# A hybrid mixing block with a mixture of experts: low parts and rotations to VectorE, convolution to GpSimd, modulation rows split over two stages

## What is computed

```python
mod = silu(c) @ w_ada + b_ada                      # 1024 -> 6 x 1024
sh1, sc1, gt1, sh2, sc2, gt2 = split(mod, 6)
h = rms_norm(x, g_mix_pre) * (1 + sc1) + sh1
proj = h @ w_in                                    # 1024 -> 3148 columns
mq, mk, mv, mo, mi, mf, aq, ak, av, iq, ik, iw = split(proj)
mq, mk = split(silu(causal_conv([mq, mk], conv_w, conv_b)))   # 4 taps, 1024 channels
hm = sigmoid(mo) * head_norm(mlstm(mq, mk, mv, mi + b_igate, mf + b_fgate))
ik = layer_norm(ik); aq, ak, iq, ik = partial_rope(...)
ha = attention over the 128 keys with the highest indexer score, causal by chunks of 64
x = x + gt1 * rms_norm([hm, ha] @ w_out, g_mix_post)
h2 = rms_norm(x, g_ffn_pre) * (1 + sc2) + sh2
x = x + gt2 * rms_norm(moe(h2), g_ffn_post)        # 64 experts, 8 per token, one shared
```

## Time and profile before

| | us |
|---|---|
| median of 3 runs | 1194.58 |
| lowest, highest | 1193.11, 1201.09 |
| the profiled execution | 1198.99 |
| its span in the profile | 1197.2 |
| DVE busy in the span | 841.9 |
| PE busy in the span | 1047.7 |
| POOL busy in the span | 408.4 |

### The profile page before, as it was taken

The page is one execution under the profiler, slowest core; times in us unless marked ns, Lnnn a source line. Parts: engine busy times, 40 slices in busy tenths (PEclk is TensorE's granted clock), DMA queues, the critical chain, the costliest instruction groups (busy, mean ns, idle before and its releaser), DMA issues. The chain is left out here.

```text
span 1197.2 us, 16021 instructions
## 1 busy us (share of the span) xinstructions
PE 1047.7 (88%) x4777; PEld 747.3 (62%) x4778; DVE 841.9 (70%) x1425; ACT 527.1 (44%) x615; POOL 408.4 (34%) x195
## 2 busy tenths in 40 slices
PE   1698997778999979999999999999999999899960
PEld 1595987735744745666666776666666666566630
DVE  4786999955624283888788887867777686676735
ACT  3323263245412113555555554554555454454522
POOL 1342495100000021454453664333434252243322
PEclk9797998878999789999999999999999899899985
DMA  9664344150040737999999999999999999999843
GB/s 358 237 216 139 101 148 142 36 194 1 1 186 6 292 122 274 378 360 334 349 348 364 339 350 322 346 340 335 329 339 333 343 341 303 319 329 315 299 103 150
DMA packets 84489, 302.93 MB, mean 253 GB/s; under 512 B 10997, under 2 KB 23329, under 8 KB 74921
## 3 DMA queue, kind: packets, MB, share of 16 engines
q1 hardware_dynamic: 70336, 263.30, 60.9%
q0 software_dynamic: 12544, 35.70, 12.9%
q10 hardware_dynamic: 1514, 2.97, 0.7%
HBM read 276.80 MB, written 27.30 MB: 254 GB/s over the span
## 5 line engine op out<-in xcount | busy, mean ns | idle before, releaser
L1720 DVE TENSOR_TENSOR w_gate_up_lo<-side,w_gate_up_hi 128x2048 fp32r<-128x2048 f32 x64 | 146.7, 2294 | 82.9 <-ACT w_gate_up_hi L1637 82.7
L1720 DVE TENSOR_TENSOR w_gate_up_lo<-main,w_gate_up_hi 128x2048 fp32r<-128x2048 f32 x64 | 146.7, 2293 | 79.6 <-ACT w_gate_up_hi L1637 79.6
L1637 ACT ACTIVATE w_gate_up_hi<-side 128x2048 fp32r<-128x2048 f32 x64 | 122.2, 1910 | 116.0 <-DMA side<-in_w_exp_up 65.7
L1637 ACT ACTIVATE w_gate_up_hi<-main 128x2048 fp32r<-128x2048 f32 x64 | 122.2, 1910 | 108.3 <-DMA main<-in_w_exp_up 53.5
L1801 PE MATMUL ps<-w_gate_up_hi,xT_hi 128*128 128x512 f32 x512 | 146.4, 408 | 13.2 <-DVE xT_lo L1724 10.2
L1480 POOL DMA_INDIRECT xg<-h_rows,row_numbers x48 | 98.6, 2055 | 173.6 <-issue 128.0
L1801 PE MATMUL ps<-w_gate_up_hi,xT_lo 128*128 128x512 f32 x512 | 139.4, 395 | 0.0
L1801 PE MATMUL ps<-w_gate_up_lo,xT_hi 128*128 128x512 f32 x512 | 138.8, 394 | 0.0
L1486 POOL DMA_INDIRECT y_rows_even<-yb,row_numbers x32 | 79.7, 2490 | 103.4 <-issue 103.4
L1801 PEld LDWEIGHTS ps<-w_gate_up_hi,xT_hi 128*128 128x128 f32 x512 | 93.2, 192 | 34.2 <-issue 15.7
L1801 PEld LDWEIGHTS ps<-w_gate_up_hi,xT_lo 128*128 128x128 f32 x512 | 97.4, 190 | 21.5
(11 more groups left out here) (294 smaller groups left out, 1751.8 us busy)
## 6 DMA issues: line engine op xcount, KB each, us to landing
side<-in_w_exp_gate SPq DMA_DIRECT2D x60, 512.0 KB, 9.9
side<-in_w_exp_up SPq DMA_DIRECT2D x60, 512.0 KB, 24.5
main<-in_w_exp_gate SPq DMA_DIRECT2D x60, 512.0 KB, 10.3
main<-in_w_exp_up SPq DMA_DIRECT2D x60, 512.0 KB, 23.5
side<-in_w_ada SPq DMA_DIRECT2D x24, 1024.0 KB, 6.9
side<-in_w_exp_down SPq DMA_DIRECT2D x16, 1024.0 KB, 24.8
main<-in_w_exp_down SPq DMA_DIRECT2D x16, 1024.0 KB, 25.0
maskb<-in_w_exp_down SPq DMA_DIRECT2D x16, 1024.0 KB, 23.9
```

The lines of the kernel that those rows point to most:

```text
L1637: nc.scalar.activation(whi[:, half], wgu[n % RING][:, :, HALF * half:HALF * (half + 1), :] .rearrange("p m c f -> p c m f"), ACT.Copy).the ...
L1720: nc.vector.tensor_tensor(wlo[:, half], src, whi[:, half].bitcast(F32), ALU.subtract).then_inc(s_wlo, 1)
```

## The change

- In-projection: low parts and rotations move from POOL to VectorE, the low parts into the rounds of the selection at places written in `low_at`. The convolution's three later taps move from VectorE to POOL, each as a product with a scalar (into the place of the result, `qkc`) and a sum; three buffers hold taps instead of two.
- The gates' work and the query turns move from the attention stage into the in-projection: turns on TensorE, scans on VectorE between rounds, exponentials and copies on ScalarE.
- TensorE's order: item 0 goes over h's chunks in the outer loop, with the low weight part second; item 3's four tiles are put between the indexer's turns and products.
- Of the four later rows of `mod` only two (8 pieces) are summed here. One piece of the third is loaded in the attention stage, seven pieces are loaded in the output stage; VectorE sums them there, four ahead of the first tile, three after the tiles and one before the routing. The row sums of TensorE are split: four halves after `scores(0)`, two after `project_out(0)`, two before the last small product.

`gates(1)` is the five instructions L846 to L850, `gates(2)` the six L870 to L877, with the same shapes (4 x 512). `modulate(n)` is `modulation` with the stage's own buffers; `products(i)` and `relu_products(i)` are the loops over heads at L670 and L416 for one i; `early_rows(a, b)` is `modulation` for those pieces.

```diff
-ROWS = [("row", s, q) for s in range(2, 5) for q in range(4)]
-LAST_ROW = [("last", 5, q) for q in range(4)]
+ROWS = [("row", s, q) for s in range(2, 4) for q in range(4)]
-STREAM = (ADA + ITEMS[0:2] + ROWS[0:2] + ITEMS[2:3] + ROWS[2:5] + ITEMS[3:5] + ROWS[5:7] + ITEMS[5:6] + ROWS[7:8] + ITEMS[6:8]
-          + LAST_ROW[0:1] + ITEMS[8:9] + LAST_ROW[1:2] + ITEMS[9:10] + ROWS[8:9] + LAST_ROW[2:3] + ITEMS[10:] + LAST_ROW[3:4]
-          + ROWS[9:])
+STREAM = (ADA + ITEMS[0:2] + ROWS[0:2] + ITEMS[2:3] + ROWS[2:4] + ITEMS[3:4] + ROWS[4:7] + ITEMS[4:5] + ROWS[7:8] + ITEMS[5:])
...
+            for c in range(2 * HEADS):
+                pool.wait_ge(s_tap, c + 1)
+                o, r, x = taps[c % 3], raw[:, c % 4, :], qkc[:, c, :]
+                for j in range(1, CONV):
+                    step(nc.gpsimd.tensor_scalar(x, r[:, j:j + SEQ], cols[:, 8 * j + c:8 * j + c + 1], None, ALU.mult))
+                    ins = nc.gpsimd.tensor_tensor(o, o, x, ALU.add)
+                    step(ins) if j < CONV - 1 else ins.then_inc(s_conv, 1)
...
+            copy_nat(3, [0, 1])
+            for i in range(1, NT):
+                relu_products(i)
+                if i + 1 < NT:
+                    copy_nat(3, [i + 1])
...
+                if c >= 3:
+                    silu_qk(c - 3)
+                first_tap(c)
                 if c % 2:
                     high_part(7 + c // 2)
...
-                        ins = nc.scalar.activation(w, w, ACT.Copy, scale=cs[:, 2 * q + b:2 * q + b + 1])
...
+                if c == 1:
+                    act.wait_ge(s_absf, 1)
+                    step(nc.scalar.activation(gt, gt, ACT.Exp, scale=-1.0))
+                    nc.scalar.activation(gt, gt, ACT.Ln, bias=1.0).then_inc(s_lse, 1)
+                if c == 5:
+                    act.wait_ge(s_em, 1)
+                    nc.scalar.activation(gt, gt, ACT.Exp, scale=-1.0).then_inc(s_emd, 1)
...
+            silu_qk(7)
             copy_nat(10)
-            silu_qk(7)
+            for h in range(HEADS + 1):
+                act.wait_ge(s_qT, h + 1)
...
+            def low_part(m):
+
+                n = KC * width(ITEMS[m])
+                dve.wait_ge(s_whi, m + 1)
+                nc.vector.tensor_tensor(wlo[:, m % 2, 0:n], stage[:, place[ITEMS[m]] % SLOTS, 0:n],
+                                        whi[:, m % 2, 0:n].bitcast(F32), ALU.subtract).then_inc(s_wlo, 1)
...
+            low_part(0)
             dve.wait_ge(s_mod, 1)
...
+            low_part(1)
             dve.wait_ge(s_bias, 48)
...
+            early_rows(0, 2)
+            low_part(2)
+            early_rows(2, 4)
...
+            rope(IQ0, IH, IDIM, ROT_I, K_COSI, K_SINI, None)
+            rope(IK0, 1, IDIM, ROT_I, K_COSI, K_SINI, s_rope)
+            early_rows(4, 7)
+            low_part(4)
+            early_rows(7, 8)
...
+            low_at = {(1, 1): 5, (1, 11): 6, (1, 15): 7, (2, 1): 8, (2, 8): 9, (2, 15): 10, (3, 8): 11}
+            gates_at = {(1, 14): 1, (2, 0): 2}
+            rope_at = (1, 10)
...
-                    if (i, r) in conv_at:
-                        conv(conv_at[i, r])
+                    if (i, r) == rope_at:
+                        dve.wait_ge(s_natd, first[5])
+                        rope(AK0, 1, DH, ROT_A, K_COSA, K_SINA, None)
+                        rope(AQ0, HEADS, DH, ROT_A, K_COSA, K_SINA, s_roped)
+                    if (i, r) in gates_at:
+                        gates(gates_at[i, r])
+                    if (i, r) in low_at:
+                        low_part(low_at[i, r])
...
+                pe.wait_ge(s_whi, 1)
+                pe.wait_ge(s_hf, NT)
+                for j, (hp, wp) in enumerate(((hhi, whi), (hhi, wlo), (hlo, whi))):
...
+            project_first()
             project(1)
             project(2)
+            project(3, [0])
+            pe.wait_ge(s_hf, KC)
...
+            project(3, [1])
             pe.wait_ge(s_iTd, NT + 1)
             for i in range(1, NT):
...
+                products(i)
+                if i + 1 < NT:
+                    project(3, [i + 1])
+            project(4)
+            project(5)
...
+            for m in range(6, 11):
                 project(m)
+            pe.wait_ge(s_emd, 1)
...
+            pe.wait_ge(s_roped, 1)
+            for h in range(HEADS + 1):
+                if h >= 3:
+                    pe.wait_ge(s_qTd, h - 2)
...
+            project(11)
...
+            sp.dma_start(G.row_piece, A["w_ada"][0].rearrange("(p c) n -> p c n", c=KC)[:, 0:2, 4 * D:5 * D]).then_inc(s_piece, 16)
...
-            finish_rows(4, 8)
...
+                if h == 0:
+                    dve.wait_ge(s_in, 16)
+                    finish_rows(0, 4)
...
-            sum_rows(0, 8)
...
+                if h == 0:
+                    sum_rows(0, 4)
...
+        PIECES = [(s, q) for s in (4, 5) for q in range(4)]
+        BUFFERS = [G.row_piece, piece2[:, :, :]]
...
+            load_piece(1)
+            for n, name in enumerate(("g_ffn_pre", "g_ffn_post")):
+                sp.dma_start(gains[:, n, :], A[name].broadcast_to([P, D])).then_inc(s_gain, 16)
+            load_piece(2)
             sp.dma_start(xt[:, :, :], A["x"][0].rearrange("(i p) d -> p i d", p=P)).then_inc(s_xin, 16)
+            load_piece(3)
...
+            for n in range(4, 8):
+                load_piece(n)
             sp.wait_ge(s_y, NT)
...
+            sp.wait_ge(s_used, 7)
...
+            for n in range(4):
+                modulate(n)
             dve.wait_ge(s_xin, 16)
+            dve.wait_ge(s_gain, 32)
+            finish_rows(0, 2)
...
+                if i < NT - 1:
+                    modulate(4 + i)
             copy_h2T(NT - 1)
+            modulate(7)
...
+            finish_rows(2, 4)
             dve.wait_ge(s_tab, 1)
...
             project_out(0)
+            pe.wait_ge(s_used, 4)
+            sum_rows(0, 2)
...
             shared(1, 1, 0, SEQ)
+            pe.wait_ge(s_used, 8)
+            pe.wait_ge(s_sco, 1)
+            sum_rows(2, 4)
             pe.wait_ge(s_dg, 1)
```

More of the change, by code:

```diff
@@ L240, in stage_in @@
         IDX_DONE = first[2]
-        freed, count = [], {"ada": 0, "row": 0, "last": 0}
+        freed, count = [], {"ada": 0, "row": 0}
         for piece in STREAM:
@@ L245, in stage_in @@
                 count[piece[0]] += 1
-                freed.append(({"row": s_row_used, "ada": s_ada_used, "last": s_last_used}[piece[0]], count[piece[0]]))
+                freed.append(({"row": s_row_used, "ada": s_ada_used}[piece[0]], count[piece[0]]))
             else:
@@ L269, in _ @@
                     sp.wait_ge(*freed[n - SLOTS])
-                if kind in ("ada", "row", "last"):
+                if kind in ("ada", "row"):
                     dst = stage[:, n % SLOTS, 0:2 * D].rearrange("p (c n) -> p c n", c=2)
@@ L385, in _, with copy_nat @@
             high_part(1)
-            def copy_nat(m):
+            def copy_nat(m, tiles=range(NT)):
                 c0, w = NAT_PIECES[ITEMS[m][1]]
-                for i in range(NT):
+                for i in tiles:
                     n = first[m] + i
@@ L531, in _ @@
             step(nc.vector.tensor_tensor(lnb[:, :, :], lnb[:, :, :], gk, ALU.mult))
-            nc.vector.tensor_tensor(ik, lnb[:, :, :], bk, ALU.add).then_inc(s_ln, 1)
-            for n, piece in enumerate(ROWS[5:7]):
-                modulation(piece, rows[:, piece[1] - 2, :], s_row_used, 5 + n)
-            dve.wait_ge(s_iw, 1)
+            step(nc.vector.tensor_tensor(ik, lnb[:, :, :], bk, ALU.add))
+            rope(IQ0, IH, IDIM, ROT_I, K_COSI, K_SINI, None)
[3 more added lines that the diff above has]
+            early_rows(7, 8)
             for i in range(1, NT):
@@ L583, in _ @@
             nc.vector.tensor_copy(maskb[:, 0, 0:P], k[:, K_CAUSAL:K_CAUSAL + P])
-            for n, piece in enumerate(ROWS[9:12]):
-                modulation(piece, rows[:, piece[1] - 2, :], s_row_used, 9 + n)
+            dve.wait_ge(s_an, 1)
+            nc.vector.tensor_copy(aN, ps[:, 6, 0:2 * NT * HEADS].rearrange("p (a i h) -> p a i h", a=2, i=NT))
         @block.tensor
@@ L617, in _, with project_first, project @@
             PARTS = ((hhi, whi), (hlo, whi), (hhi, wlo))
-            def project(m):
+            def project_first():
+                w = width(ITEMS[0])
+                pe.wait_ge(s_whi, 1)
+                pe.wait_ge(s_hf, NT)
+                for j, (hp, wp) in enumerate(((hhi, whi), (hhi, wlo), (hlo, whi))):
+                    wt = wp[:, 0, 0:KC * w].rearrange("p (c n) -> p c n", c=KC)
+                    for c in range(KC):
+                        pe.wait_ge((s_hhi, s_wlo, s_hlo)[j], (c + 1, 1, c + 1)[j])
+                        for i in range(NT):
+                            ins = nc.tensor.matmul(ps[:, i, 0:w], hp[:, c, i * P:(i + 1) * P], wt[:, c, :],
+                                                   start=j == 0 and c == 0, stop=j == 2 and c == KC - 1)
+                            if j == 2 and c == KC - 1:
```

(10 more changed lines are left out.)

333 lines of the change are left out of this document (147 added, 186 removed).

## The result

The changed kernel took 1182.82 us (median of 4 runs, 1178.53 to 1183.87) beside 1196.03 for the kernel before (4 runs); the ratio is 0.9878, with a 95% interval of 0.9835 to 0.9921. That is 13.2 us or 1.2% less. The prediction said 1165, 29 us less than the 1194.58 measured until then (31 less than 1196.03): the direction and the range held, the size was over twice what came.

What follows compares the result with a forecast made beforehand. VectorE was taken to bound the in-projection's later part, TensorE the output stage and the experts. Terms -27 (in-projection), -16 (attention), +14 (output) gave -29 from 1198.99, 1170; the median 4.4 lower, so 1165 us, range 1146 to 1185.

Steps and rivals of the forecast that it cites:

- In-projection, second half: In-projection from the selection's start: VectorE ends it at 212 instead of 239.1, -27 us, with GpSimd's convolution done near 191.
- the copy: GpSimd's copy, 1.89 us for 2048 elements, from which 0.5 was the lower bound for the convolution's product.
- signs of being wrong: GpSimd TENSOR_SCALAR over 1 us, VectorE's middle low parts over 4 each, TensorE waiting for SiLU or copy_nat(10) at the end.
- Rival (a): In-projection: GpSimd's convolution is the bound, product 1.2 us, stage ends at 223; sum -18, 1176 us; chance 0.15.
- three stalls that the contention was argued from: In-projection, VectorE: an hT_lo subtraction of 5.24 us (median 0.68), three convolution steps 10.31 (another channel 2.33), two row sums 9.18.
- First half: In-projection up to the selection: item 0 ends at about 57 instead of 67.4, selection starts at 105 instead of 115.8.
- Attention: Attention stage: the head of 16.5 us and a wait of 1.66 go, four row sums (3.5) come in; net -16 us.
- Output stage: Output projection: TensorE idles 8 us for piece 3, then row sums and half rate; net +14 us (+8 to +20).
- (b): In-projection: no contention worth the name between VectorE and GpSimd, stage ends at 199; sum -47, 1148 us; chance 0.14.
- (c): In-projection: the lock makes VectorE and GpSimd wait for each other; slower from 12.7 us per channel, 1207 at 14.2; chance 0.04.
- (d): Output stage: moved rows eat the gain, their sums chaining on every load, +20 or more; about 1187 us; chance 0.07.

Runs made afterwards that it cites:

- the run with GpSimd idle: The changed kernel with the convolution back on VectorE and low parts 9, 10 and 11 one to seven rounds earlier: 1172.89 us, ratio 0.9809.

## Why the prediction was right or wrong

**The step that failed** is the price of GpSimd's TENSOR_SCALAR in "In-projection, second half": "above, 1.2 as the two-input sum. I take 0.6 (one input, as the copy)". It measured 1.57, outside both bounds. The bound went wrong by the thought that one input can't cost more than two. With it a channel was 10.45 us instead of 8.6 (6.1 and VectorE's blocks), the eighth ended at 207.9 instead of 191, and TensorE, not VectorE, ended the stage, 17.1 us of it standing behind ScalarE's SiLU and copies. The prediction's own signs of being wrong named it: a TENSOR_SCALAR over 1 us, and TensorE waiting for SiLU. The Trainium skill (GPSIMD Engine Reference, "Engine selection") calls one-input work there roughly line-rate, by the prediction's estimate 0.43 us for this one; the trace has 1.57, or 1.49 with a constant, and does not bear it out for this operation.

**Rival (a) is what happened**: it said that the eighth channel ends at 206 and TensorE 17 us behind it, 223; it was 207.9 and 226.6 (18.7 behind). That its channel of 10.4 us met the measured 10.45 is luck: its product was too cheap (1.2 for 1.57, 1.1 us a channel), and VectorE held GpSimd up for 1.4 us a channel (80.2 busy, less 24 products and sums of 2.86) where the forecast had 2.5. Its chance of 0.15 was too low. Its reason ("the copy" speaks against) rested on an instruction of another kind, and for the engine that was given the work no row priced the operation.

**The rest of that stage held.** With the two-input product, at 1.04 inside the forecast's bounds, it ended at 212.8 (forecast 212), VectorE and TensorE within 1 us of each other. Low parts 8 to 11 were done at 154.4, 166.2, 178.0 and 197.5 (forecast 153.5, 165, 177, 196). The stretch of VectorE's instructions there is 13.5 us against the run with GpSimd idle (3.6 in the low parts, 9.8 in gates and closings); 13 was predicted. In the changed kernel itself it is only 5 to 6; why it is less beside the slower form was not tried. MAX8 took 0.56 (384 keys) and 0.69 (512) in every company, as said. Of the three stalls that the contention was argued from, has GpSimd's instruction beside the one at 174.1 only; the trace has it at the others too (a low part from 50.67 to 55.60, low parts and row sums from 158.11 on).

**First half.** The selection began at 106.95, predicted 105; item 0 ended at 58.1, predicted 57; `hT_lo` took 4.90 instead of 9.45 with GpSimd idle. Right in its times; the low parts' own share of the 9 us is 1 to 3.

**Attention**: -20.4 for -16. The head of 16.5 went. Of the 4 us beyond it, 3.3 lie ahead of the first product with `vext`, and a term stands there that the prediction did not have: this part ran at the half rate before and no longer does. First before, then after:

```profile
267.75 4.80 PE L1026 MATMUL ps<-main 128*128 128x512 f32 x8
```
```profile
231.87 4.54 PE L993 MATMUL ps<-rows,consts 128*128 128x512 f32 x8
...
237.39 2.91 PE L1007 MATMUL ps<-main 128*128 128x512 f32 x8
```

The first broadcast is 1.8 us shorter (1.95 for 3.78), the wait of 1.66 is gone, and two heads' scores and the second broadcast give 4.1. Against that stand the four row sums that moved in: they took 4.5 us of TensorE's time (3.5 forecast), and were paid for by the faster clock (granted 0.93 in the stage, 0.83 before).

**Output stage**: +14.4 for +14, and by its parts too: a wait of 9.5 (8 forecast), sums of 3.8 (1.8 and the half rate) and half a microsecond of slow matmuls behind. From the first product to the router's it is 74.6 us (297.1 to 371.7), 13.9 longer than before; the last two sums add 1.9, and 1.4 comes back elsewhere, nearly all of it in the router's products (9.18 for 10.50).

**Rivals (b) to (d).** (b) is out, since contention cost VectorE up to 13.5 us. (c) asked for 12.7 us per channel and 10.45 came; the point at which the change loses was not far. (d) is half right in kind: the late pieces did chain on a load, at the +14 that the forecast had.

With the product in a form that costs 1.04, near enough to the 0.6 for the convolution to end at 195.3, the kernel took 1167.8, for 1165 predicted.

## What to carry to other kernels

Before work goes to another engine, price the very instruction there, its form included; where no row has it, bound it from above by more than its nearest relative, for fewer inputs need not be cheaper. A long wait that one engine passes on to TensorE costs twice, once as idle time and once as the slow matmuls behind it (after 11.2 us here the first eight took 2.10 instead of 1.13, after 1.6 us 1.22). What is loaded for a chain of uses is issued ahead of bulk that nobody needs yet, and the seven pieces moved to the output stage then cost 0.6 us of VectorE's work and loads, beside TensorE's row sums.

## What the runs showed of the hardware

- GpSimd, 128x512 f32: product with one scalar for each partition 1.57 us, with a constant 1.49, product of two inputs (one read over and over from one column) 1.04, sum of two inputs 1.29.
- VectorE's steps waited for a running GpSimd instruction, one with a single input (TENSOR_SCALAR, 0.41 us became 3.97) and one with two (TENSOR_TENSOR, 0.42 became 4.83), and GpSimd's product for VectorE's low parts (1.04 became 3.0). MAX8 and MATCH_REPLACE8 never did, nor did the gates' first step, which reads its input from a TensorE bank (0.74 at 130.98, beside a low part on GpSimd from 130.84 to 135.44). The Trainium skill (SBUF — State Buffer, "SBUF: two separate sides") names the pair of ports that the two share as an exclusive lock for a whole instruction; the trace agrees. Seven GpSimd instructions of 4.6 to 5.0 us (33 us in all) stretched VectorE's work by 23, forty-eight short ones (69 us) by 13.5; VectorE's work beside them was not the same.
- The same 1 MB piece was used 5.0 us after its issue with nothing ahead of it and 13 us after with up to 4 MB ahead.
